# Two key heads joined into one attention item, and the softmax scale folded into the transposes

## The chip, the cores and the metric

The kernel runs on one core of a Trainium2 chip. The metric is the device time of one execution in microseconds (us). Everything is float32.

## The reference, cut to what matters

The reference is a chain of three transformer blocks over 512 tokens of width 1024: a gated delta net, a retention block, and a block whose mixer is half HGRN2 and half a sparse attention, each followed by a convolutional feed-forward layer. Only the sparse attention (`nsa`) is touched. It has 8 query heads in 2 key heads (groups) of 4, each 64 wide. Every query head attends over three branches and the results are summed with a gate for each:

```
s     = einsum(q, k_cmp) * scale                   # branch 0: 31 compressed keys
p_cmp = softmax(where(cvalid, s, NEG)) * any_valid
o_cmp = p_cmp @ v_cmp
o_slc = softmax(causal(q @ k_s * scale)) @ v_s     # branch 1
o_win = softmax(causal(q @ k_w * scale)) @ v_w     # branch 2
o     = g0 * o_cmp + g1 * o_slc + g2 * o_win
```

With 512 tokens all 8 blocks are selected and the window covers everything, so branches 1 and 2 are plain causal attention over 512 keys.

## The kernel before, in words

The program is one straight-line list of instructions for each engine (TensorE, VectorE, ScalarE, GpSimd), ordered by hand. Every engine counts its finished steps in one semaphore, and another engine waits until that count has reached the number of a named step (`at("act", "nsa", "exp", n)`); there is no planner. Activations are held transposed: features on the 128 partitions, tokens along the free axis. Weights come through a ring of three slots filled by the SyncE queue; the attention stage below reads none of them.

The attention stage is written in `pe_nsa`, `act_nsa` and `dve_nsa`. Its queries lie in `NX[half(g), r, :]`: key head g = 0 on partitions 0-63 and g = 1 on 64-127, four query heads r in each. The work after the compression is a list of 72 items `ITEMS = (r, g, b, i)`: for each of 4 r and 2 g, one item of the compressed branch (b = 0, all 4 blocks of 128 queries at once) and four each of branches 1 and 2, one per block i of 128 queries, which sees (i+1)*128 keys. An item goes round the engines:

- TensorE, `scores` (L1936 for b = 0, L1939 else): queries (64 rows by 128) as weights, keys streamed, into one of four banks in rotation, up to 3 items ahead.
- VectorE, `front` (L2068 to L2071, or L2074): mask, and the maximum of each row. For b > 0 one instruction and a read of its accumulator.
- ScalarE, `exp` (L2002, L2004): the exponential into `Pn`, for b > 0 with the row sum.
- VectorE (L2087 to L2092, or L2095 and L2097): the reciprocal, then the whole row times reciprocal times gate. L2097 writes (i+1)*128 columns.
- TensorE (L1969): one transpose per 128 keys, into bank 2 or 3.
- ScalarE (L2016, L2018): the copy of that bank into `PTn`.
- TensorE, `values` (L1951, L1954): `VSW` or `VCMP` (128 or 31 rows by 64 columns) as weights, `PTn` streamed, into `O[half(g)]`, partitions 0-63 or 64-127 of one bank for each r, where the three branches add up.

In TensorE's queue the order within one turn n is `scores(n+3)`, transposes of n, `values(n-1)`. VectorE does `front(n+1)` before the scaling of n, and ScalarE `exp(n+1)` before the copy of n. When the 9 items of a head pair are done, `dve_o` (L2117) copies the bank into `HT`. A float32 matmul is two passes through the array (two MATMUL instructions, each with its own weight load); a transpose is one. After the stage comes `mix_out` (L267), a projection with weights already in the ring.

Of the kernel before, what the change touches and what calls it, by code (L numbers as in the profile page):

```python
# [7 lines left out]
ALU = mybir.AluOpType  # L8
# [78 lines left out]
def program(nc, dr, out, plan):  # L87
# [3 lines left out]
    with ExitStack() as ctx:  # L91
# [22 lines left out]
        def at(*name):  # L114
            return plan.get(name, 1)
# [1750 lines left out]
        o = work + 6 * T  # L1866
        KCMP = region(o, 32); o += 32
        VCMP = region(o, 2, ND); o += 2 * ND
        assert o <= 21504
        Pn = [region(work + m * T, T) for m in range(3)]  # L1870
        PTn = [region(work + (3 + m) * T, T) for m in range(2)]
        tri = region(work + 5 * T, T)
        SB = (0, 1, 6, 7)
# [3 lines left out]
        ITEMS = [(r, g, b, i) for r in range(4) for g in range(NG) for b, i in [(0, 0)] + [(b, i) for b in (1, 2) for i in range(NT)]]  # L1877

        def half(g):
            return slice(ND * g, ND * g + ND)  # L1880

        def pe_nsa(pe):
# [47 lines left out]
            def scores(n):  # L1930
                r, g, b, i = ITEMS[n]
                if n >= 4:
                    pe.wait_ge(act_done, at("act", "nsa", "exp", n - 4))
                if b == 0:
                    for i in range(NT):
                        last = nc.tensor.matmul(B4[SB[n % 4]][:, i, 0:NCMP], NX[half(g), r, i * P:(i + 1) * P], KCMP[half(g), 0:NCMP],  # L1936
                                                start=True, stop=True)
                else:
                    last = nc.tensor.matmul(B[SB[n % 4]][:, 0:(i + 1) * P], NX[half(g), r, i * P:(i + 1) * P],  # L1939
                                            NX[half(g), 5 + b, 0:(i + 1) * P], start=True, stop=True)  # L1940
                last.then_inc(pe_done, PE.tick("nsa", "score", n))

            def values(n):

                r, g, b, i = ITEMS[n]
                pe.wait_ge(act_done, at("act", "nsa", "pt", n))
                O = B[4 + r % 2]
                if b == 0:
                    if g == 0 and r >= 2:
                        pe.wait_ge(dve_done, at("dve", "nsa", "o", r - 2))  # L1950
                    last = nc.tensor.matmul(O[half(g), :], VCMP[0:NCMP, g, :], PTn[n % 2][0:NCMP, :], start=True, stop=True)  # L1951
                else:
                    for j in range(i + 1):
                        last = nc.tensor.matmul(O[half(g), i * P:(i + 1) * P], VSW[:, j, (b - 1) * P + g * ND:(b - 1) * P + (g + 1) * ND],  # L1954
                                                tiles(PTn[n % 2])[:, j, :], start=False, stop=True, skip_group_check=True)
                last.then_inc(pe_done, PE.tick("nsa", "pv", n))
# [3 lines left out]
            scores(2)  # L1960
            for n, (r, g, b, i) in enumerate(ITEMS):
                if n + 3 < len(ITEMS):
                    scores(n + 3)
                pe.wait_ge(dve_done, at("dve", "nsa", "p", n))
                if n >= 2:
                    pe.wait_ge(act_done, at("act", "nsa", "pt", n - 2))
                p4 = tiles(Pn[n % 3])
                for j in range(NT if b == 0 else i + 1):
                    last = nc.tensor.transpose(B4[2 + n % 2][:, j, :], p4[:, j, :], ident[:, :])  # L1969
                last.then_inc(pe_done, PE.tick("nsa", "pt", n))  # L1970
                if n:
                    values(n - 1)
# [3 lines left out]
        def act_nsa(act):  # L1976
# [19 lines left out]
            def exp(n):  # L1996
                r, g, b, i = ITEMS[n]
                act.wait_ge(dve_done, at("dve", "nsa", "max", n))
                if n >= 3:
                    act.wait_ge(pe_done, at("pe", "nsa", "pt", n - 3))  # L2000
                if b == 0:
                    ins = nc.scalar.activation(tiles(Pn[n % 3])[:, :, 0:NCMP], B4[SB[n % 4]][:, :, 0:NCMP], ACT.Exp, scale=SCALE)  # L2002
                else:
                    ins = nc.scalar.activation(Pn[n % 3][:, 0:(i + 1) * P], B[SB[n % 4]][:, 0:(i + 1) * P], ACT.Exp, scale=-1.0,  # L2004
                                               bias=small[:, 20 + n % 3:21 + n % 3], accum_out=small[:, 40 + n % 3:41 + n % 3])
                ins.then_inc(act_done, AC.tick("nsa", "exp", n))

            exp(0)
            for n, (r, g, b, i) in enumerate(ITEMS):
                if n + 1 < len(ITEMS):  # L2010
                    exp(n + 1)
                act.wait_ge(pe_done, at("pe", "nsa", "pt", n))
                if n >= 2:
                    act.wait_ge(pe_done, at("pe", "nsa", "pv", n - 2))
                if b == 0:
                    ins = nc.scalar.activation(PTn[n % 2][0:NCMP, :], B[2 + n % 2][0:NCMP, :], ACT.Copy)  # L2016
                else:
                    ins = nc.scalar.activation(PTn[n % 2][:, 0:(i + 1) * P], B[2 + n % 2][:, 0:(i + 1) * P], ACT.Copy)  # L2018
                ins.then_inc(act_done, AC.tick("nsa", "pt", n))
            AC.mark("end", "nsa")  # L2020

        def dve_nsa(dve):
# [29 lines left out]
            for m in range(3):  # L2052

                nc.vector.memset(Pn[m], 0.0).then_inc(dve_done, DV.tick())
# [3 lines left out]
            cm = cmask[:, :, 0:NCMP]  # L2058

            def front(n):  # L2060

                r, g, b, i = ITEMS[n]
                dve.wait_ge(pe_done, at("pe", "nsa", "score", n))
                if n >= 3:
                    dve.wait_ge(act_done, at("act", "nsa", "exp", n - 3))
                if b == 0:
                    S = B4[SB[n % 4]][:, :, 0:NCMP]
                    step(nc.vector.tensor_tensor(S, S, cm, ALU.add))  # L2068
                    step(nc.vector.reduce_max(small[:, 24:28], S, AX))
                    m4 = small[:, 24:28].rearrange("p (i o) -> p i o", o=1).to_broadcast([P, NT, NCMP])  # L2070
                    nc.vector.tensor_tensor(S, S, m4, ALU.subtract).then_inc(dve_done, DV.tick("nsa", "max", n))  # L2071
                else:
                    S = B[SB[n % 4]]
                    nc.vector.tensor_tensor_reduce(out=S[:, 0:(i + 1) * P], in0=S[:, 0:(i + 1) * P], in1=tri[:, (3 - i) * P:4 * P],  # L2074
                                                   scale=-SCALE, scalar=3e38, op0=ALU.add, op1=ALU.min,
                                                   accum_out=small[:, 20 + n % 3:21 + n % 3]).then_inc(dve_done, DV.tick("nsa", "max", n))

            front(0)
            for n, (r, g, b, i) in enumerate(ITEMS):
                if n + 1 < len(ITEMS):  # L2080
                    front(n + 1)
                dve.wait_ge(act_done, at("act", "nsa", "exp", n))
                head = NG * 2 * g + r
                if b == 0:
                    Pc = tiles(Pn[n % 3])[:, :, 0:NCMP]
                    s4 = small[:, 32:36]
                    step(nc.vector.reduce_sum(s4, Pc, AX))  # L2087
                    step(nc.vector.reciprocal(s4, s4))
                    step(nc.vector.tensor_tensor(s4, s4, cmask[:, :, 31:32].rearrange("p i o -> p (i o)"), ALU.mult))
                    step(nc.vector.tensor_tensor(s4, s4, VSW[:, :, 256 + 3 * head], ALU.mult))  # L2090
                    w4 = s4.rearrange("p (i o) -> p i o", o=1).to_broadcast([P, NT, NCMP])
                    nc.vector.tensor_tensor(Pc, Pc, w4, ALU.mult).then_inc(dve_done, DV.tick("nsa", "p", n))  # L2092
                else:
                    s = small[:, 36 + n % 2:37 + n % 2]
                    step(nc.vector.reciprocal(s, small[:, 40 + n % 3:41 + n % 3]))  # L2095

                    nc.vector.tensor_scalar(Pn[n % 3][:, 0:(i + 1) * P], Pn[n % 3][:, 0:(i + 1) * P], s,  # L2097
                                            VSW[:, i, 256 + 3 * head + b:257 + 3 * head + b], ALU.mult, ALU.mult)\
                        .then_inc(dve_done, DV.tick("nsa", "p", n))
                if g == 1 and b == 0 and r:  # L2100
                    dve_o(dve, r - 1)
# [11 lines left out]
        def dve_o(dve, r):  # L2113

            last_item = max(n for n, item in enumerate(ITEMS) if item[0] == r)
            dve.wait_ge(pe_done, at("pe", "nsa", "pv", last_item))
            nc.vector.tensor_copy(HT[:, 4 + r, :], B[4 + r % 2][:, :]).then_inc(dve_done, DV.tick("nsa", "o", r))  # L2117
# [342 lines left out]
```

## Time and profile before

| | us |
|---|---|
| median of 3 runs | 3148.64 (3146.46 to 3150.63) |
| the profiled execution | 3151.16 |
| its span, first to last instruction | 3149.3 |
| TensorE busy in the span | 2975.5 (94%) |
| VectorE, ScalarE busy | 1561.0, 643.6 |
| mean granted TensorE clock | 0.934 |

Lines of code are named L1939 and so on. A group of the profile is all instructions of one line, engine and shape, with its busy time, the mean duration of one, and the idle time of the engine before them. A granted clock of 1.00 is 2.4 GHz for TensorE, 0.50 is 1.2 GHz. A matmul's record is longer than the time for which it holds the array, since one begins before the record of the last one ends; so the distance from start to start is what counts.

### The profile page before, as it was taken

The page shows a single profiled execution, that of the slowest core. Times are in us where ns is not written, and L with a number is a line of the kernel's source. Part 1 is how long each engine was busy: PE and PEld are TensorE (multiplying, and loading weights), DVE is VectorE, ACT ScalarE, POOL GpSimd, SP SyncE. Part 2 cuts the span into 40 slices and gives each one's busy share as a digit, 9 for nine tenths or more (in the row PEclk, how much of TensorE's full clock was granted, in tenths as well). Part 3 has the DMA queues.
Part 4 walks back from the last instruction along what each step waited for, and adds up shares of the span by engine and source line. Part 5 has one row for each costly group of instructions (what it writes and reads, how often), then busy time and mean ns, then how long its engine had stood idle before and what let it go on. Part 6 is the DMA issues. An engine that isn't in the chain of part 4 may idle for free. (4 is left out here: it accounts for less than half of the span.)

```text
span 3149.3 us, 29504 instructions
## 1 busy us (share of the span) xinstructions
PE 2975.5 (94%) x11724; PEld 2053.1 (65%) x11724; DVE 1561.0 (50%) x2776; ACT 643.6 (20%) x1124; POOL 149.6 (5%) x118
## 2 busy tenths in 40 slices
PE   6999999889999999999899999979998999999999
PEld 5666666648888854444346888854454555488888
DVE  3555565537777520222116776646564333366652
ACT  1112211112111010111102111024535222122200
POOL 0000000001000010000001000001230000000000
PEclk9998999899999999999899999989998555999999
DMA  7112111122443321211122444320113000122221
GB/s 291 37 58 89 67 54 54 54 80 107 164 176 125 138 90 54 84 57 57 53 80 80 167 178 146 128 90 30 68 54 134 1 1 1 54 81 80 91 92 46
DMA packets 24488, 274.96 MB, mean 87 GB/s; under 512 B 3480, under 2 KB 4376, under 8 KB 7072
## 3 DMA queue, kind: packets, MB, share of 16 engines
q1 hardware_dynamic: 19440, 266.45, 22.8%
q10 hardware_dynamic: 4912, 6.63, 0.6%
q8 instruction: 94, 1.54, 0.2%
q14 instruction: 42, 0.34, 0.0%
HBM read 270.97 MB, written 2.10 MB: 87 GB/s over the span
## 5 line engine op out<-in xcount | busy, mean ns | idle before, releaser
L323 PE MATMUL bank<-HT,ring 128*128 128x256 f32 x1056 | 257.7, 389 | 20.1 <-ACT HT L671 12.7
L939 PE MATMUL bank<-HT,ring 128*128 128x512 f32 x512 | 261.0, 640 | 0.0
L323 PE MATMUL bank<-arena 128*128 128x256 f32 x1056 | 249.5, 379 | 0.0
L323 PE MATMUL bank<-arena,ring 128*128 128x256 f32 x1056 | 249.5, 379 | 0.0
L323 PEld LDWEIGHTS bank<-HT,ring 128*128 128x128 f32 x1056 | 204.1, 195 | 51.7 <-issue 23.3
L323 PEld LDWEIGHTS bank<-arena 128*128 128x128 f32 x1056 | 200.6, 190 | 27.3
L323 PEld LDWEIGHTS bank<-arena,ring 128*128 128x128 f32 x1056 | 200.6, 190 | 27.3
L400 PE MATMUL bank<-arena,ring 128*128 128x256 f32 x936 | 207.5, 380 | 5.5 <-ACT arena L470 3.9
L267 PE MATMUL bank<-arena,ring 128*128 128x512 f32 x448 | 198.2, 602 | 10.3 <-issue 7.9
L400 PEld LDWEIGHTS bank<-arena,ring 128*128 128x128 f32 x936 | 177.0, 190 | 30.9 <-ACT arena L470 5.1
L244 DVE SCALAR_TENSOR_TENSOR arena<-ring,evec,arena 128x512 f32<-128x512 f32 x224 | 167.3, 747 | 3.8
L267 PEld LDWEIGHTS bank<-arena,ring 128*128 128x128 f32 x448 | 86.5, 194 | 120.5 <-issue 119.4
L1535 PE MATMUL bank<-HT,ring 128*128 128x512 f32 x320 | 148.1, 600 | 4.3 <-ACT HT L699 4.3
L860 ACT ACTIVATE arena<-bank,ffc 128x512 f32<-128x512 f32 x66 | 51.3, 777 | 471.3 <-DVE bank L788 471.3
L939 PEld LDWEIGHTS bank<-HT,ring 128*128 128x128 f32 x512 | 95.4, 205 | 79.0 <-issue 79.0
L323 PE MATMUL bank<-HT,arena 128*128 128x256 f32 x528 | 126.4, 382 | 0.2
L1355 PE MATMUL bank<-ring,HT 128*128 128x512 f32 x256 | 114.7, 608 | 8.2 <-ACT arena L660 8.2
L1336 PE MATMUL bank<-HT,ring 128*128 128x512 f32 x256 | 112.9, 602 | 6.3 <-ACT HT L671 6.3
L400 PE MATMUL bank<-arena 128*128 128x256 f32 x528 | 116.4, 379 | 0.0
L1369 PE MATMUL bank<-HT,ring 128*128 128x512 f32 x256 | 110.5, 592 | 0.0
L323 PEld LDWEIGHTS bank<-HT,arena 128*128 128x128 f32 x528 | 98.6, 190 | 18.2 <-DVE arena L838 5.7
L400 PEld LDWEIGHTS bank<-arena 128*128 128x128 f32 x528 | 100.3, 190 | 13.6
(395 smaller groups left out, 4203.8 us busy)
## 6 DMA issues: line engine op xcount, KB each, us to landing
ring<-w_ada SPq DMA_DIRECT2D x33, 2048.0 KB, 8.0
ring<-w_up SPq DMA_DIRECT2D x33, 2048.0 KB, 7.8
ring<-w_down SPq DMA_DIRECT2D x24, 1408.0 KB, 6.0
ring<-w_gdn SPq DMA_DIRECT2D x8, 2048.0 KB, 12.4
ring<-w_ret_qk SPq DMA_DIRECT2D x4, 2048.0 KB, 8.0
ring<-w_ret_v SPq DMA_DIRECT2D x4, 2048.0 KB, 7.9
ring<-w_ret_g SPq DMA_DIRECT2D x4, 2048.0 KB, 7.8
ring<-w_ret_out SPq DMA_DIRECT2D x4, 2048.0 KB, 7.9
```

What stands on the lines that cost most here:

```text
L244: ins = nc.vector.scalar_tensor_tensor(out=acc, in0=w[:, :, k, :], scalar=evec[:, e, k:k + 1], in1=acc, op0=ALU.mult, op1=ALU.add)
L267: last = nc.tensor.matmul(bank[:, :], w[:, n % per_load, k, :], src(k), start=(k == 0), stop=(k == kc - 1))
L323: last = nc.tensor.matmul(out_, w[:, k, :], x[:, k, :], start=(first and k == 0), stop=(k == 3), skip_group_check=not first)
L400: last = nc.tensor.matmul(out_, w[:, k, :], x(k), start=(first and k == 0), stop=(k == KH2 - 1), skip_group_check=not first)
L860: nc.scalar.activation(ffn_y[:, j % 2, :], B[j % 2][:, :], ACT.Identity, scale=ffc[:, i, j, 0, 2:3], bias=ffc[:, i, j, 0, 3:4])\
L939: last = nc.tensor.matmul(B[u % 2][:, :], w[:, u, k, :], HT[:, k, :], start=(k == 0), stop=(k == KC - 1))
L1336: last = nc.tensor.matmul(B[X + u][:, :], w[:, u, k, :], HT[:, k, :], start=(k == 0), stop=(k == KC - 1))
L1355: last = nc.tensor.matmul(B[Y + i][:, :], HT[:, k, i * P:(i + 1) * P], w[:, k, :], start=(k == 0), stop=(k == KC - 1))
L1369: last = nc.tensor.matmul(B[Y + u][:, :], w[:, u, k, :], HT[:, k, :], start=(k == 0), stop=(k == KC - 1))
L1535: last = nc.tensor.matmul(bank[:, :], w[:, u, k, :], HT[:, k, :], start=(k == 0), stop=(k == KC - 1))
```

## The change: what it does

Items become `(r, b, i)`, 36 of them, each for both key heads. Scores of the two heads are issued one after the other from rows 0-63 and 64-127 into two banks, up to 2 items ahead; two pairs of banks alternate. The values of the two heads are issued alternately into bank 4, partitions 0-63, and bank 5, partitions 64-127, and these two banks now serve every r. For b > 0 VectorE no longer scales the rows of `Pn`: it scales the identity (128 by 128) by reciprocal times gate into one of six tiles `scale_n`, and TensorE multiplies `Pn` by that diagonal matrix instead of transposing it, which transposes and scales at once. The copies into `PTn`, the exponentials and the maxima stay one instruction per key head. `dve_o` copies two halves of 64 partitions.

```diff
-        SB = (0, 1, 6, 7)
+        scale_n = [region(o + m * P, P) for m in range(6)]; o += 6 * P
+        SB = ((0, 1), (6, 7))
-        ITEMS = [(r, g, b, i) for r in range(4) for g in range(NG) for b, i in [(0, 0)] + ...]
+        ITEMS = [(r, b, i) for r in range(4) for b, i in [(0, 0)] + ...]
...
             def scores(n):
-                if n >= 4:
-                    pe.wait_ge(act_done, at("act", "nsa", "exp", n - 4))
+                if n >= 2:
+                    pe.wait_ge(act_done, at("act", "nsa", "exp", n - 2, 1))
...
+                    for g in range(NG):
+                        last = nc.tensor.matmul(B[SB[n % 2][g]][:, 0:(i + 1) * P], NX[half(g), r, i * P:(i + 1) * P],
+                                                NX[half(g), 5 + b, 0:(i + 1) * P], start=True, stop=True)
...
             def values(n):
+                pe.wait_ge(act_done, at("act", "nsa", "pt", n, 1))
                 if b == 0:
+                    if r:
+                        pe.wait_ge(dve_done, at("dve", "nsa", "o", r - 1))
...
                     for j in range(i + 1):
+                        for g in range(NG):
+                            last = nc.tensor.matmul(B[4 + g][half(g), i * P:(i + 1) * P], VSW[:, j, (b - 1) * P + g * ND:(b - 1) * P + (g + 1) * ND],
+                                                    PTn[n % 2][:, g, j * P:(j + 1) * P], start=False, stop=True, skip_group_check=True)
...
+            for n, (r, b, i) in enumerate(ITEMS):
+                if n + 2 < len(ITEMS):
+                    scores(n + 2)
+                for g in range(NG):
+                    pe.wait_ge(dve_done, at("dve", "nsa", "p", n, g))
+                    if n:
+                        pe.wait_ge(act_done, at("act", "nsa", "pt", n - 1, g))
+                    for j in range(NT if b == 0 else i + 1):
+                        if b == 0:
+                            last = nc.tensor.transpose(B4[2 + g][:, j, :], Pn[n % 3][:, 4 * g + j, :], ident[:, :])
+                        else:
+                            last = nc.tensor.matmul(B4[2 + g][:, j, :], Pn[n % 3][:, 4 * g + j, :], scale_n[2 * (n % 3) + g], start=True, stop=True)
...
# VectorE, after the exponentials
+                dve.wait_ge(act_done, at("act", "nsa", "exp", n, 1))
...
-                    nc.vector.tensor_scalar(Pn[n % 3][:, 0:(i + 1) * P], Pn[n % 3][:, 0:(i + 1) * P], s,
-                                            VSW[:, i, 256 + 3 * head + b:257 + 3 * head + b], ALU.mult, ALU.mult)
+                    step(nc.vector.reciprocal(small[:, c:c + 2], small[:, c:c + 2]))
+                    for g in range(NG):
+                        nc.vector.tensor_scalar(scale_n[2 * (n % 3) + g], ident[:, :], small[:, c + g:c + g + 1],
+                                                VSW[:, i, 256 + 3 * head + b:257 + 3 * head + b], ALU.mult, ALU.mult)
...
-            nc.vector.tensor_copy(HT[:, 4 + r, :], B[4 + r % 2][:, :])
+            nc.vector.tensor_copy(HT[half(0), 4 + r, :], B[4][half(0), :])
+            nc.vector.tensor_copy(HT[half(1), 4 + r, :], B[5][half(1), :])
```

## Rows read from the trace of the kernel before

**Rows 1.** The page: granted clock of TensorE in 40 equal slices, in tenths.
```profile
PEclk9998999899999999999899999989998555999999
```
**Rows 2.** Stretches: length, busy us (count) of each engine, clock, DMA share, GB/s.
```profile
2434.00:2679.00 245.00, 243.47 (x721) 137.16 (x721) 90.89 (x325) 68.24 (x211) 0.00 (x0) 0.52 0.01 3
```
**Rows 3.** Groups of 2434.2 to 2679.5 by shape, TensorE's matmuls.
```profile
L1954 PE MATMUL bank<-arena 128*64 128x128 f32 x320 | 82.4, 422 | 0.0
L1969 PE MATMUL bank<-ident,arena 128*128 128x128 f32 x192 | 58.1, 430 | 0.2 <-DVE arena L2097 0.2
...
L1939 PE MATMUL bank<-arena 64*128 64x512 f32 x32 | 31.9, 1096 | 0.0
...
L1936 PE MATMUL bank<-arena 64*128 64x31 f32 x64 | 15.3, 400 | 0.4 <-ACT arena L1993 0.4
```
**Rows 4.** Timeline at the low clock: start, length, engine, line, operation, count.
```profile
2453.35 2.07 PE L1939 MATMUL bank<-arena 64*128 64x512 f32 x2
...
2455.35 0.47 PE L1969 MATMUL bank<-ident,arena 128*128 128x128 f32 x1
...
2455.75 1.97 PE L1954 MATMUL bank<-arena 128*64 128x128 f32 x8
...
2457.65 1.91 PE L1936 MATMUL bank<-arena 64*128 64x31 f32 x8
...
2459.50 0.69 PE L1969 MATMUL bank<-ident,arena 128*128 128x128 f32 x2
```
**Rows 5.** Timeline of TensorE where shapes alternate and nothing is waited for.
```profile
2432.15 0.64 PE L1925 MATMUL bank<-w2c,arena 128*31 128x64 f32 x4
2432.72 0.64 PE L1923 MATMUL bank<-arena,w2c 128*64 128x31 f32 x4
```
**Rows 6.** Timeline of TensorE about the first rise of the clock.
```profile
2500.13 1.11 PE L1969 MATMUL bank<-ident,arena 128*128 128x128 f32 x4
2501.17 1.97 PE L1954 MATMUL bank<-arena 128*64 128x128 f32 x8
...
2504.64 1.07 PE L1951 MATMUL bank<-arena 31*64 31x512 f32 x2
2505.64 0.48 PE L1939 MATMUL bank<-arena 64*128 64x128 f32 x2
2506.05 0.44 PE L1969 MATMUL bank<-ident,arena 128*128 128x128 f32 x2
2506.42 0.43 PE L1954 MATMUL bank<-arena 128*64 128x128 f32 x2
2506.78 1.00 PE L1939 MATMUL bank<-arena 64*128 64x256 f32 x2
```
**Rows 7.** Stretches before, in and after that rise, and one of the delta net.
```profile
2500.20:2503.60 3.40, 3.40 (x13) 2.71 (x14) 1.20 (x4) 1.03 (x3) 0.00 (x0) 0.50 0.00 0
2503.80:2507.00 3.20, 3.20 (x12) 1.23 (x11) 1.67 (x6) 1.31 (x5) 0.00 (x0) 1.00 0.00 0
2507.20:2510.60 3.40, 3.40 (x11) 1.72 (x9) 1.62 (x6) 1.22 (x5) 0.00 (x0) 0.50 0.00 0
...
600.00:626.00 26.00, 19.63 (x151) 17.54 (x149) 21.34 (x40) 0.65 (x2) 0.10 (x1) 1.00 0.01 2
```
**Rows 8.** Group of 600 to 626, TensorE: the stretch's products.
```profile
L1026 PE MATMUL bank<-arena 128*128 128x128 f32 x48 | 6.4, 277 | 0.8 <-DVE arena L1251 0.8
```
**Rows 9.** Timeline of TensorE at the stage's end, after the last scores.
```profile
2671.11 1.97 PE L1954 MATMUL bank<-arena 128*64 128x128 f32 x8
...
2674.73 0.65 PE L1954 MATMUL bank<-arena 128*64 128x128 f32 x4
```
**Rows 10.** Groups of VectorE and ScalarE, 2434.2 to 2679.5.
```profile
L2074 DVE CUSTOM_DVE_ANT_0 bank<-bank,arena 128x512 f32<-128x512 f32 x16 | 11.2, 699 | 28.9 <-PE bank L1939 28.9
L2004 ACT ACTIVATE arena<-bank,small 128x512 f32<-128x512 f32 x16 | 10.9, 681 | 0.0
...
L2097 DVE TENSOR_SCALAR arena<-arena,small 128x128 f32<-128x128 f32 x16 | 5.5, 346 | 0.6
```

More of the change, by code:

```diff
@@ L1865, in program @@
         assert o <= 4 * HH * T
-        o = work + 6 * T
+        o = work
+        Pn = [region(o + m * 2 * T, 2 * NT, P) for m in range(3)]; o += 6 * T
+        PTn = [region(o + m * 2 * T, 2, T) for m in range(2)]; o += 4 * T
+        tri = region(o, T); o += T
         KCMP = region(o, 32); o += 32
         VCMP = region(o, 2, ND); o += 2 * ND
[L1869 to L1872, printed above, removed]
-        SB = (0, 1, 6, 7)
+        scale_n = [region(o + m * P, P) for m in range(6)]; o += 6 * P
+        assert o <= 26000, o
+        SB = ((0, 1), (6, 7))
         NORMED = [4, 0, 1, 2, 3, 6, 7]
@@ L1876, in program @@
         SCALE = ND ** -0.5
[L1877 removed]
+        ITEMS = [(r, b, i) for r in range(4) for b, i in [(0, 0)] + [(b, i) for b in (1, 2) for i in range(NT)]]
         def half(g):
@@ L1959, in pe_nsa @@
             scores(1)
[L1960 to L1970, printed above, removed]
+            for n, (r, b, i) in enumerate(ITEMS):
+                if n + 2 < len(ITEMS):
+                    scores(n + 2)
+                for g in range(NG):
+                    pe.wait_ge(dve_done, at("dve", "nsa", "p", n, g))
[6 more added lines that the diff above has]
+                            last = nc.tensor.matmul(B4[2 + g][:, j, :], Pn[n % 3][:, 4 * g + j, :], scale_n[2 * (n % 3) + g], start=True, stop=True)
+                    last.then_inc(pe_done, PE.tick("nsa", "pt", n, g))
                 if n:
@@ new lines, in front @@
+                    S = [B4[SB[n % 2][g]][:, :, 0:NCMP] for g in range(NG)]
+                    m4 = [small[:, 24 + 4 * g:28 + 4 * g] for g in range(NG)]
+                    for g in range(NG):
+                        ins = nc.vector.tensor_tensor(S[g], S[g], cm, ALU.add)
+                    step(ins)
+                    for g in range(NG):
+                        ins = nc.vector.reduce_max(m4[g], S[g], AX)
+                    step(ins)
+                    for g in range(NG):
+                        nc.vector.tensor_tensor(S[g], S[g], m4[g].rearrange("p (i o) -> p i o", o=1).to_broadcast([P, NT, NCMP]), ALU.subtract)\
+                            .then_inc(dve_done, DV.tick("nsa", "max", n, g))
+                else:
+                    for g in range(NG):
+                        S, c = B[SB[n % 2][g]], 2 * (n % 2) + g
+                        nc.vector.tensor_tensor_reduce(out=S[:, 0:(i + 1) * P], in0=S[:, 0:(i + 1) * P], in1=tri[:, (3 - i) * P:4 * P],
+                                                       scale=-SCALE, scalar=3e38, op0=ALU.add, op1=ALU.min,
+                                                       accum_out=small[:, 20 + c:21 + c]).then_inc(dve_done, DV.tick("nsa", "max", n, g))
@@ L2078, in dve_nsa @@
             front(0)
[L2079 removed]
+            for n, (r, b, i) in enumerate(ITEMS):
                 if n + 1 < len(ITEMS):
                     front(n + 1)
[L2082 to L2083 removed]
+                dve.wait_ge(act_done, at("act", "nsa", "exp", n, 1))
                 if b == 0:
[L2085 to L2092, printed above, removed]
[L2093 to L2100 removed]
@@ new lines, in dve_nsa @@
+                    Pc = Pn[n % 3][:, :, 0:NCMP]
+                    s8 = small[:, 32:40]
+                    step(nc.vector.reduce_sum(s8, Pc, AX))
+                    step(nc.vector.reciprocal(s8, s8))
+                    for g in range(NG):
+                        s4 = s8[:, 4 * g:4 * g + 4]
+                        step(nc.vector.tensor_tensor(s4, s4, valid, ALU.mult))
+                        step(nc.vector.tensor_tensor(s4, s4, VSW[:, :, 256 + 3 * (NG * 2 * g + r)], ALU.mult))
+                        w4 = s4.rearrange("p (i o) -> p i o", o=1).to_broadcast([P, NT, NCMP])
+                        nc.vector.tensor_tensor(Pc[:, 4 * g:4 * g + 4, :], Pc[:, 4 * g:4 * g + 4, :], w4, ALU.mult)\
+                            .then_inc(dve_done, DV.tick("nsa", "p", n, g))
+                else:
+                    c = 40 + 2 * (n % 2)
+                    step(nc.vector.reciprocal(small[:, c:c + 2], small[:, c:c + 2]))
+                    for g in range(NG):
+                        head = NG * 2 * g + r
+                        nc.vector.tensor_scalar(scale_n[2 * (n % 3) + g], ident[:, :], small[:, c + g:c + g + 1], VSW[:, i, 256 + 3 * head + b:257 + 3 * head + b],
+                                                ALU.mult, ALU.mult).then_inc(dve_done, DV.tick("nsa", "p", n, g))
@@ L2101, in dve_nsa @@
+                if b == 1 and i == 0 and r:
                     dve_o(dve, r - 1)
```

70 lines of the change are left out of this document (29 added, 41 removed).

## The prediction, made before the changed kernel ran

> **What bounds the kernel now.** I read four views in this order. First the page: TensorE is busy 94% of the span (the table above), and its granted clock is near full except in three of the 40 slices, where it is about a half [rows 1]. Those slices are the attention stage. Second the stage as one stretch: in the 245 us from 2434 to 2679 TensorE is busy 243.5, VectorE 90.9, ScalarE 68.2, the DMA engines nearly nothing, and the clock stands at 0.52 [rows 2]. So TensorE bounds the stage, at 1.2 GHz, and a wait of another engine costs nothing as long as TensorE has other work. Third the groups, which give counts: 320 value passes, 192 transposes, 128 score passes (32 of each width), 64 and 16 passes of the compressed branch [rows 3]. Fourth the timeline of single items, which gives prices.
>
> Price of a pass, at the low clock. One transpose takes 0.47 and two 0.69, eight value passes 1.97 [rows 4]: (1.97 - 0.47) / 7 = 0.214 us for each further pass of 128 columns. I call that a unit; 512 columns are four units. At the high clock two passes take 0.43 [rows 6] and four 0.65 [rows 9]: a unit is 0.11. A record's rest is a tail that overlaps what follows.
>
> Price of a change of shape, from start to start. One transpose to the values behind it: 0.40 - 0.21 = 0.19. Eight value passes to the scores: 1.90 - 1.71 = 0.19. Score passes of 512 to the transpose: 2.00 - 1.71 = 0.29 [rows 4]. That is 0.67 us for each item, which goes round scores, transposes, values. It is not the price of a wait: where shapes alternate and nothing is waited for, four passes of 64 columns (0.43) take 0.57 until the next shape begins [rows 5]. At the high clock the three are 0.19, 0.15 and 0.14 [rows 6]: 0.48.
>
> Does this add up to the stage? The 64 items of branches 1 and 2 hold 320 units of scores, 320 of values, 160 of transposes: 800 x 0.214 = 171. Changes: 64 x 0.67 = 43. A compressed item costs 1.85 (its eight score passes, start to start [rows 4]) + 0.86 + 1.71 + 0.38 for two changes = 4.8, and 8 of them 38. Sum 252 for 245 measured; the stretches in which the clock was up [rows 7, 9] make up the difference.
>
> **The change part by part.** What it does to TensorE is counted in units, since it is the bound.
>
> Scores. Each key head's two passes stay, on half of the rows. If the two halves run side by side, head 0's second pass lies beside head 1's first, and a pair costs three passes where it cost four: 240 units for 320. If not, 320. The trace before never has two half-height or half-width tiles next to each other without another shape between, so both ends stay; I take the overlap, since the two use different rows and banks.
>
> Values. The two heads alternate, each on 64 columns of its own bank: 2(i+1)+1 passes for 4(i+1) if side by side, 192 units for 320. If not, 320. I take the overlap for the same reason; the side that costs stays in the range. The Trainium skill (TensorEngine Tiling (Array Packing), Key Properties) states that different tiles run in parallel and that changing the tiling mode drains the engine. The second half agrees with the 0.19 to 0.29 above; no run here shows the first.
>
> Transposes. 160 one-pass transposes become 160 two-pass products: 320 units for 160. This is a loss for certain, unless it buys something else.
>
> Changes of shape. 36 items for 72. The second key head's transposes wait for two more semaphores, but in the same shape. In the old trace waiting weight loads in one shape cost nothing visible when their count was reached long before, so I price them at nothing; at the other end they cost a change each, 36 x 0.19 = 7 us. What is queued behind them is the values of n-1, and ScalarE's copies wait for those products.
>
> Compressed items: 16 score passes that load weights more than they stream, 1.85 x 2 = 3.7 at the low clock (I assume that the halves save nothing here; at best half), 8 transposes, and 12 units of values (16 without overlap).
>
> VectorE. The rescaling of whole rows (16 each of 0.35 to 0.55, 28.6 us by the four shapes) becomes 64 tiles of 128 columns at 0.346 [rows 10] = 22.1. 32 reciprocals go, at 0.16 each, 5 us; the halved copies `dve_o` double, 4 x 0.69 more, and 0.7 of it is exposed at the end. VectorE stays near 82 us, ScalarE at 68. The three memsets of `Pn` are twice as long, some 1.6 us, before the first maximum, beside the first two scores; if that cover is gone it costs 1.6.
>
> Sum at the low clock: 240 + 192 + 320 = 752 units x 0.214 = 161; changes 32 x 0.67 = 21; compressed items 4 x (3.7 + 1.7 + 2.6 + 0.5) = 34. That is 216, 29 us less than 245. Without overlap it is 960 x 0.214 + 21 + 4 x 9.3 = 264, 19 us more.
>
> **The clock.** This term is larger than all the others. TensorE is busy without a gap, and still at 1.2 GHz. So the trace shows that being busy is not what brings the high clock; I looked at what ran before it changed. The first rise, just after 2503.6, follows four transposes and eight value passes, all on 128 rows [rows 6, 7]. It lasts some 3.4 us, in which 31-row and 64-row passes run [rows 6], and by 2507.2 the clock is down again [rows 7]. At the stage's end, once no scores are left and only values and transposes run, it is up too: four value passes take 0.65 there, where eight took 1.97 just before [rows 9]. Elsewhere, products of 128x128x128 on all rows hold 1.00 over 26 us in which TensorE is busy just 19.6 [rows 7, 8]. What keeps this stage at the low clock is then its share of passes on half of the rows, 320 of 800 units, and the changes between shapes.
>
> The change moves both. Transposes are 320 of its units, values 192 to 320, all on 128 rows; scores fall to 240, in a third of which both halves are at work; and half of the changes go. I take it that the clock rises within the first few items and, since full-height work at twice the speed held it elsewhere with a quarter of the time idle, stays.
>
> Sum at the high clock: 752 x 0.11 = 83; changes 32 x 0.48 = 15; compressed items 4 x (1.9 + 0.9 + 1.3 + 0.3) = 18 with rounding up for weight loads. That is 116. To it: the first items at the low clock, 10 us instead of 5, +5; a fall at the compressed items, whose scores and values stream 31 columns or rows, +1 each, +4; and waits. TensorE now needs some 116 us where VectorE needs 82 and its small gaps, so it is covered less. The chain from a pair's scores to its products is two maxima of 0.70, an exponential of 0.68, its sum, a reciprocal and two tiles of 0.35 [rows 10], about 3.3 us, against two turns of TensorE work, 1.6 us each for one block and 4.6 for four. It is exposed after short items only: I take 8 for the 36 items. With the 0.7 at the end: 134.
>
> The stage goes from 245 to 134: -111. The profiled execution, 3151.2, becomes 3040; it lies 2.5 above the median of the runs, so the median becomes 3038.
>
> The Trainium skill (TensorE: Matmul & The Clock Gate, Part 4: PE-mode transpose) says that transposes do not bring the high clock. The trace agrees only in part: the rise after 2503.6 came behind four transposes and eight value passes, and whether the values alone did it cannot be read. By that rule replacing transposes with products is what matters, and the sum would be the same 134.
>
> **The rivals.**
>
> Overlap fails, clock rises. 960 units x 0.11 = 106, + 15 + 4 x 4.8 = 140, + 18 = 158: median 3062. For it: no row shows two halves at once. Against: they share neither rows nor banks, or neither columns nor banks.
>
> The clock swings. The compressed items and the waits pull it down for part of each head, say four tenths of the stage: between 134 and 216, near 170: 3074. For it: the fall by 2507.2 came with 31- and 64-row passes [rows 6, 7]. Against: that was one short run of them.
>
> The clock stays low, halves overlap: 216, 3120. For it: the stage stands at 0.52 now, and the scores remain on half rows.
>
> The slower one: the clock stays low and the halves run one after the other, so the second pass of each of the 160 products is paid in full. 264 us, +19: 3168. If each change of half costs as much as a change of shape (32 + 28 in the scores, 132 in the values, 192 x 0.19 = 36), 300 us: 3203. The second passes cost 160 x 0.214 = 34 us and fewer changes give back 24 (36 x 0.67), so it decides from the point at which the overlap gives less than 10 of the 45 us (208 units) that I count for it. Rows 5 speak for it, since width changes there cost time without a wait; against it, that is another shape, not another half of one.
>
> That the change doesn't do what it says (run halves side by side) is the first rival and this last one.
>
> **How the numbers follow.** Forecast (high clock, overlap) 0.58; high clock without overlap 0.14; swinging clock 0.10; low with overlap 0.08; low without, slower, 0.08; no change within 0.2% 0.02, where losses and gains meet. What a measurement of this kernel can tell from no change is about 0.2%, 6 us. Faster 0.90, same 0.02, slower 0.08. The time is the forecast's, 3038. Its own bounds: waits and falls at nothing (118 + 5) give 3025, twice what I took gives 3055. The range holds these, the case without overlap and the swinging clock: 3020 to 3105.
>
> **What would show it.** Right: the stage about 134 us long; its clock over 0.9 after the first 10 us; 752 units, so that starts of the two heads' passes coincide; L1939's second head begins before the first head's second pass ends; the L1969 products twice as many and 0.11 apart; VectorE busy near 82. Wrong: the clock at 0.50 in the products; records of the two heads end to end; TensorE idle behind VectorE for more than a tenth of the stage, or a changed stage after 2679.

## The result, and the profile after

The changed kernel takes 3016.17 us (median of 4 runs, 3010.99 to 3020.42), the kernel before 3149.64 beside it: a ratio of 0.9577, with a 95% interval of 0.9556 to 0.9598. A second measurement of the same kernel on another occasion gave 3016.32 and again 0.9577 (0.9557 to 0.9598). The forecast was 3038 with a range of 3020 to 3105: right in direction, cause and order of size, but the gain was 133 us and not 111, and the time lies 4 us below the range. (Of the four runs the profiled one took 3012.24, some 4 us under the median; the stage below is read from it.)

The page of the changed kernel: the span, the busy time, and the granted clock in 40 slices. The three slices at a half of before [rows 1] are gone.

```profile
span 3010.4 us, 29648 instructions
...
PE 2834.6 (94%) x11884; PEld 1993.0 (66%) x11884; DVE 1542.0 (51%) x2740; ACT 642.8 (21%) x1124; POOL 149.6 (5%) x118
...
PEclk9999999899999999999989999999899999999999
```

The stage runs from its first score at 2432.0 to the first pass of the projection at 2539.7. As stretches (length, then busy time and count of TensorE, its weight loads, VectorE, ScalarE, GpSimd; clock; DMA), whole, its first 10 us, and the rest without its end:

```profile
2432.00:2539.70 107.70, 103.57 (x880) 74.77 (x880) 71.72 (x291) 67.15 (x209) 0.00 (x0) 0.96 0.01 5
2432.00:2442.00 10.00, 8.36 (x44) 5.50 (x44) 7.77 (x34) 5.61 (x18) 0.00 (x0) 0.60 0.10 43
2442.00:2534.00 92.00, 91.11 (x792) 65.83 (x792) 62.58 (x256) 60.06 (x191) 0.00 (x0) 1.00 0.01 2
```

It was 244.6 us at a clock of 0.52 [rows 2, between the same two passes]. That is 137 us less, and the spans differ by 139; from the stage's end to the last instruction the two take 470 us each. The whole gain lies in the stage. TensorE still bounds it: it is busy 91 of 92 us, at the full clock.

TensorE's groups in the stage by shape (count, busy us, mean ns; idle before). They answer to [rows 3]: the products are twice the passes, the others are as many as before but are busy for less than a third of the time.

```profile
L1976 PE MATMUL bank<-arena 128*128 128x128 f32 x320 | 44.2, 285 | 0.6 <-DVE arena L2120 0.5
L1959 PE MATMUL bank<-arena 128*64 128x128 f32 x320 | 24.4, 283 | 0.0
L1943 PE MATMUL bank<-arena 64*128 64x512 f32 x32 | 9.0, 641 | 0.0
```

The timeline of TensorE (start, length, line, shape, count), in which the passes of both heads stand in one row:

```profile
2473.21 2.05 PE L1976 MATMUL bank<-arena 128*128 128x128 f32 x16
2475.19 0.88 PE L1959 MATMUL bank<-arena 128*64 128x128 f32 x12
2476.00 0.92 PE L1943 MATMUL bank<-arena 64*128 64x384 f32 x4
2476.84 0.71 PE L1976 MATMUL bank<-arena 128*128 128x128 f32 x4
2477.49 1.09 PE L1959 MATMUL bank<-arena 128*64 128x128 f32 x16
2478.51 1.13 PE L1943 MATMUL bank<-arena 64*128 64x512 f32 x4
```

Sixteen value passes take 1.09 us, twelve 0.88 and, elsewhere in the stage, four 0.44: (1.09 - 0.88) / 4 = 0.053 for a further pass, half of 0.11. Both heads' passes run all the way side by side. In the single records the first two passes of every such group start 6 to 8 ns apart, in the values and in the scores, and the third 0.16 us or more later. Passes of one half never start so close together (0.109 us apart, in the run with grouped values below), so each of these pairs is one pass of head 0 and one of head 1. The four score passes of 512 columns take 1.13, where two took 2.07 at the low clock [rows 4]. The sixteen products take 2.05, at 0.11 each.

### The profile page after: what moved, and what is told of

Read it like the earlier page. It is cut to its first block and busy times, and to the rows that moved or that the text cites. A ratio compares the mean times of both kernels' runs of the same rounds, so it can differ in the third digit from the quotient of the medians.

```text
span 3010.4 us, 29648 instructions
## 1 busy us (share of the span) xinstructions
PE 2834.6 (94%) x11884; PEld 1993.0 (66%) x11884; DVE 1542.0 (51%) x2740; ACT 642.8 (21%) x1124; POOL 149.6 (5%) x118
## 5 line engine op out<-in xcount | busy, mean ns | idle before, releaser
L323 PE MATMUL bank<-HT,ring 128*128 128x256 f32 x1056 | 258.1, 390 | 20.1 <-ACT HT L671 12.7
L400 PEld LDWEIGHTS bank<-arena 128*128 128x128 f32 x528 | 100.3, 190 | 13.6
```

The lines of the kernel that those rows point to most:

```text
L323: last = nc.tensor.matmul(out_, w[:, k, :], x[:, k, :], start=(first and k == 0), stop=(k == 3), skip_group_check=not first)
L400: last = nc.tensor.matmul(out_, w[:, k, :], x(k), start=(first and k == 0), stop=(k == KH2 - 1), skip_group_check=not first)
```

## The experiments

Stage lengths are from the first score pass to the first pass of the projection, in the profiled execution. The part of the program ahead of the stage differs by up to 8 us from one profiled execution to another, while the stage of two kernels that were profiled twice came out the same within 0.1 us, so the stage is the finer measure. In the executions shown the clock falls 1 to 3 us before the stage begins. The fifth column is the length of that first stretch at the low clock, the last one all the time at the low clock within the stage.

| kernel | time, us | ratio to before | stage, us | first low stretch, us | low in the stage, us |
|---|---|---|---|---|---|
| before | 3149 | 1 | 244.6 | 72 | 233 |
| changed | 3016 | 0.9577 | 107.7 | 10 | 8 |
| one half at a time | 3091 | 0.983 | 182.9 | 38 | 63 |
| values grouped | 3015 | 0.959 | 113.9 | 10 | 9 |
| joined, transposes | 2998 | 0.954 | 95.0 | 10 | 8 |
| one head, product | 3083 | 0.980 | 184.8 | 44 | 53 |
| one head, scores on all rows | 3038 | 0.964 | 134.5 | 10 | 8 |
| scores one half at a time | 3057 | 0.970 | 158.0 | 34 | 63 |
| joined, transposes, interleaved | 3002 | 0.953 | 96.6 | 10 | 7 |
| joined, transposes, split wait | 3006 | 0.954 | 97.0 | 10 | 8 |

**One head per item, scores on all 128 rows.** This is the kernel before; only the keys lie in tiles whose other half is zero, so that a score pass uses all rows.

```diff
-    last = nc.tensor.matmul(B[SB[n % 4]][:, 0:(i + 1) * P], NX[half(g), r, i * P:(i + 1) * P],
-                            NX[half(g), 5 + b, 0:(i + 1) * P], start=True, stop=True)
+    last = nc.tensor.matmul(B[SB[n % 4]][:, 0:(i + 1) * P], NX[:, r, i * P:(i + 1) * P],
+                            KZ[:, 2 * g + b - 1, 0:(i + 1) * P], start=True, stop=True)
...
+    ins = nc.vector.tensor_copy(KZ[half(g), 2 * g + b - 1, :], NX[half(g), 5 + b, :])
...
+    ins = nc.gpsimd.memset(KZ[half(1 - g), 2 * g:2 * g + 2, :], 0.0)
```

> The kernel before, one key head per item, plain transposes; the scores of branches 1 and 2 run over all 128 rows, queries of both heads against a key tile whose other half is zero (same result, same number of passes and of columns; four half copies on VectorE, 3 us, and zeros from GpSimd). Theory (the passes on half of the rows are what keeps the clock low): it rises within 10 to 40 us and stays; 800 units x 0.11 + 64 items at about 0.35 for changes (scores and transposes now have one shape) + 8 compressed items at 3 = 135, and up to 20 for the start and waits: stage 140 to 160 us, time 3045 to 3065. Rival (it is the mere mix of short groups, or the transposes): clock near 0.5, only the changes save, 64 x 0.2 = 13 us, about 3140.

Measured: 3037.89 us, ratio 0.9637 (0.9621 to 0.9654). Its stage as stretches:

```profile
2428.50:2563.00 134.50, 133.07 (x720) 86.17 (x720) 89.10 (x328) 67.96 (x210) 0.00 (x0) 0.97 0.01 4
2436.50:2560.00 123.50, 123.00 (x684) 79.44 (x683) 82.50 (x305) 64.03 (x200) 0.00 (x0) 1.00 0.00 1
```

The same 720 matmuls as before, none shared, no product and no joining, and the stage falls from 245 to 134.5 us: 110 of the 137. The clock reads 1.00 from 2436.5 on. The edit also takes away one change of shape in three, since scores and transposes now have the same; at the low clock that is at most 64 x 0.29 = 19 us [rows 4]. The rest, 91 us, is the clock. The theory stands, and the run did better than it gave: the stage is 5 us below its 140 to 160, the time 7 us below its 3045 to 3065, and the clock was up after 8 us where it gave 10 to 40. The run doesn't fill the rows alone, since that one change of shape goes with it; what the changes of shape do for the clock is taken up below.

**One head per item, diagonal product.** The kernel before with only the product put in, for branches 1 and 2; the compressed branch keeps its transposes.

```diff
...
-    last = nc.tensor.transpose(B4[2 + n % 2][:, j, :], p4[:, j, :], ident[:, :])
+    last = nc.tensor.matmul(B4[2 + n % 2][:, j, :], p4[:, j, :], scale_n[n % 3], start=True, stop=True)   # b > 0
...
-    nc.vector.tensor_scalar(Pn[n % 3][:, 0:(i + 1) * P], Pn[n % 3][:, 0:(i + 1) * P], s,
+    nc.vector.tensor_scalar(scale_n[n % 3], ident[:, :], s,
...
```

> The kernel before, items of one key head, with only the diagonal product in place of scaling the rows and transposing. Theory (passes on all rows lift the clock, and the 160 more units are such): clock rises in the first items and stays, 960 units x 0.11 + 64 changes at 0.48 + 8 compressed items at about 3 = 160 to 175 us, time about 3070. Rival (it takes the joined halves to lift the clock): clock near 0.5, 245 + 34 = about 279 us, time about 3183.

Measured: 3082.53 us, ratio 0.980 (0.976 to 0.984). The stage up to the rise, then two stretches behind it:

```profile
2432.30:2475.30 43.00, 42.97 (x129) 27.84 (x130) 14.65 (x59) 11.34 (x33) 0.00 (x0) 0.50 0.03 14
2475.40:2598.20 122.80, 122.80 (x671) 79.94 (x670) 64.61 (x249) 50.69 (x159) 0.00 (x0) 1.00 0.00 1
...
2598.30:2608.50 10.20, 10.20 (x34) 6.81 (x33) 2.67 (x11) 2.94 (x9) 0.00 (x0) 0.50 0.00 1
```

160 passes more than before, nothing shared, and still 66 us faster. TensorE works without a gap in both stretches: 129 matmuls in the 43 us at the low clock, 671 in 122.8 at the high one, 3.0 and 5.5 in a us. The clock came, as the theory said, but after 43 us and not in the first items, and it fell once more for 10 us, so the stage was 185 us, not 160 to 175.

**Joined items, plain transposes.** The changed kernel with the scale put back on the rows.

```diff
-    last = nc.tensor.matmul(B4[2 + g][:, j, :], Pn[n % 3][:, 4 * g + j, :], scale_n[2 * (n % 3) + g], start=True, stop=True)
+    last = nc.tensor.transpose(B4[2 + g][:, j, :], Pn[n % 3][:, 4 * g + j, :], ident[:, :])
...
-    nc.vector.tensor_scalar(scale_n[2 * (n % 3) + g], ident[:, :], small[:, c + g:c + g + 1],
+    row = Pn[n % 3][:, 4 * g:4 * g + i + 1, :].rearrange("p j c -> p (j c)")
+    nc.vector.tensor_scalar(row, row, small[:, c + g:c + g + 1],
...
```

> Joined items as in the change, but the scale put on the rows by VectorE and plain one-pass transposes on TensorE as before the change. Theory (what lifts the clock is passes on all 128 rows, transposes among them, two halves at once counting as all rows): clock over 0.9, 160 units fewer on TensorE (-17.6 us), VectorE 9 us more and a longer wait for it, stage between 93 and 108, time 3001 to 3016. Rival (the product, being no transpose, is what lifts the clock): clock near 0.5, 480 units x 0.214 + 21 for changes + 25 for compressed items = about 149, time about 3057.

Measured: 2998.45 us, ratio 0.9536 (0.9508 to 0.9563). Its stage, and who waits in it (in total, times, longest):

```profile
2433.30:2528.30 95.00, 85.03 (x721) 53.44 (x721) 76.70 (x291) 65.16 (x209) 0.00 (x0) 0.96 0.02 6
2441.50:2520.00 78.50, 72.89 (x630) 44.60 (x626) 65.48 (x251) 57.26 (x190) 0.00 (x0) 1.00 0.01 1
```

```profile
PEld bank L1973 <- DVE arena L2118: 14.9, 23, 1.3
...
PE bank L1973 <- DVE arena L2118: 5.3, 8, 1.1
```

The clock is high without a single product, so the product is not needed to lift it. The stage lies within the 93 to 108 us of the theory, the time 3 us below its 3001. With the product the stage is 12.7 us longer than with the transposes it replaced: with transposes TensorE is busy 18.5 us less, but idle for 10.0 us and not 4.1, since it waits more for VectorE, which is busy 5 us more. This kernel is the fastest tried, so it was measured again beside the changed one.

> Joined items with one-pass transposes and VectorE scaling the rows, once more. Theory (the product's 160 second passes are 17.6 us of TensorE, of which VectorE's longer scaling gives 5 back): 12 to 13 us less than the changed kernel beside it (stage 95 against 108), about 3003. Rival (the difference of the first runs was the chip's): within 5 us of it.

> The changed kernel once more, beside the joined items with transposes, on one chip. Expected: 0.9577 of the kernel before, as first measured, about 3016, stage 108 us. If the time swings by more than 5 us between chips, the difference to the other one is what counts.

Measured: 2999.90 (2995.53 to 3007.57) with transposes and 3016.32 (3009.49 to 3018.25) for the changed kernel; the ratios are 0.9532 (0.9510 to 0.9554) and 0.9577 (0.9557 to 0.9598), the stages 95.0 and 107.8. 16 us less at the median, 13 in the stage.

**One half at a time.** Head 1's passes wait for the end of head 0's, in scores and values of branches 1 and 2.

```diff
     last = nc.tensor.matmul(B[SB[n % 2][g]][:, 0:(i + 1) * P], NX[half(g), r, i * P:(i + 1) * P],
                             NX[half(g), 5 + b, 0:(i + 1) * P], start=True, stop=True)
+    if g == 0:
+        last.then_inc(pe_done, PE.tick("nsa", "half"))
+        pe.wait_ge(pe_done, PE.n)
...
-    for j in range(i + 1):          # values
-        for g in range(NG):
+    for g in range(NG):
+        for j in range(i + 1):
...
+        if g == 0:                  # the same wait after head 0
...
```

> The changed kernel, but TensorE waits for head 0's passes to end before it issues head 1's, in the scores and in the values of branches 1 and 2 (values grouped by head). Theory (the two heads truly share the array, which makes 160 units of each pass count instead of 320): 320 units more at 0.11 us = 35, and 64 waits for the end of a half at about 0.35 each = 22, so the stage goes from 108 to about 165 us and the time from 3016 to about 3073. Rival (the gain is the clock and the fewer changes of shape, the overlap is worth little): the waits alone, 22, about 3038. Both expect the high clock.

Measured: 3090.67 us, ratio 0.983 (0.979 to 0.986), 75 us more than the changed kernel where 57 were expected; the stage is 75.2 us longer. The waits cost less than their price: at the high clock head 1's first pass starts 0.33 us after a last pass of 128 columns and 0.65 after one of 512, 0.21 more than a pass that follows at once, so 64 of them are 14 us and not 22. What the expectation left out is the clock, which it had left high:

```profile
2427.90:2464.00 36.10, 35.06 (x110) 21.52 (x110) 13.20 (x56) 11.77 (x36) 0.00 (x0) 0.50 0.04 15
2464.00:2528.80 64.80, 63.23 (x377) 41.35 (x375) 30.09 (x123) 26.61 (x87) 0.00 (x0) 1.00 0.00 1
2528.90:2542.50 13.60, 13.37 (x40) 8.17 (x40) 3.42 (x15) 4.12 (x14) 0.00 (x0) 0.50 0.00 0
```

It stayed low for 36 us and fell twice more, 13.6 us each time: 63 us of the stage against 8 in the changed kernel. Work at the low clock takes about twice as long, so 55 us more of it cost an estimated 27, and 35 + 14 + 27 = 76 is what was measured. Sharing the array does two things, then: it halves the passes and it keeps all rows at work.

**Scores one half at a time.** The same wait in the scores alone; the values still share.

> The changed kernel, with head 1's scores alone waiting for head 0's to end (values still share). Theory (both heads' first passes start together, so sharing saves half of 320 units, not a quarter): 160 units more, 17.6 us, and 32 waits at about 0.4, 13 us, so +31 us, about 3047, if the clock stays high; up to 15 us more if it falls for longer at the start. Rival (sharing saves a quarter, 80 units, as the prediction had it): 9 + 13 = +22 us, 3038. The trace tells them apart by the starts.

Measured: 3057.40 us in two runs, ratio 0.970 (0.968 to 0.972), so 41 us more than the changed kernel, the stage 50 us longer. That is more than both prices gave, and again it is the clock: it was low for the first 32 us of the stage and three times in all, 63 us together (the third stretch, of 13.7 us, isn't shown).

```profile
2430.70:2462.90 32.20, 31.28 (x102) 18.86 (x103) 13.06 (x56) 10.60 (x32) 0.00 (x0) 0.50 0.04 15
...
2486.90:2503.80 16.90, 16.79 (x71) 12.46 (x70) 4.75 (x21) 5.88 (x18) 0.00 (x0) 0.50 0.00 1
```

With what the runs measured, the size speaks for the half. A wait costs 0.21 here too, not 0.4, so 32 of them are 7 us, and the 55 us more at the low clock some 27, as above. With 160 units (17.6 us) that gives 52, with 80 units 43; the stage is 50.3 us longer. The starts in the changed kernel, 6 to 8 ns apart from the first pass on, say the same without an estimate.

This run and the one before it spend the same 63 us at the low clock, though the values share the array here and not there. So it is the scores one half of the rows at a time that cost the clock; values on all rows and one half of the columns at a time didn't add to it.

**Values grouped by head.** The two loops of the values change places, nothing else.

```diff
-    for j in range(i + 1):
-        for g in range(NG):
+    for g in range(NG):
+        for j in range(i + 1):
```

> The changed kernel with the values issued head by head (all blocks of head 0, then all of head 1) and not alternately, no wait added. If TensorE starts passes in the order of issue, as the prediction had it, only one pass of each item is shared: 4(i+1)-1 instead of 2(i+1) passes, 128 units more, +14 us, about 3030. If its queue can take head 1's passes ahead of head 0's by any distance, nothing changes: 3016. A short look-ahead (two or three passes) gives a value between, near the first.

Measured: 3015.13 us, ratio 0.9589 (0.9562 to 0.9616), no different from the changed kernel; the stage is 6.2 us longer. Its value passes:

```profile
2473.81 1.14 PE L1959 MATMUL bank<-arena 128*64 128x128 f32 x12
...
2476.37 1.58 PE L1959 MATMUL bank<-arena 128*64 128x128 f32 x16
```

Sixteen passes take 1.58 where they took 1.09 alternating and would take 1.97 or so one by one (sixteen at 0.11 and the tail). Head 1's first pass starts 0.49 us after head 0's first, when five of its eight have started. Where head 0 has six passes it starts when three have started, and where it has four or two, behind the first. So the engine doesn't start passes in the order of issue: it takes one for the other half ahead, over three passes at most in this kernel. The third expectation is the nearest: the stage's +6 lies between 0 and 14, if not near the upper end.

**Two orders of VectorE, on top of the joined items with transposes.** Interleaved: maximum of head 0 of the next item, scaling of head 0, maximum of head 1, scaling of head 1 (where neither item is compressed), and each scaling waits for its own exponential and has its own reciprocal.

> Joined items with transposes (the earlier experiment, stage 95 us, TensorE idle 20 us behind VectorE's scaling). VectorE's order changed: maximum of head 0 of the next item, scaling of head 0, maximum of head 1, scaling of head 1. Theory (the scaling comes late because two maxima of up to 0.7 stand ahead of it and it waits for both exponentials): up to 10 of the 20 us come back, less 5 us of VectorE for 32 more reciprocals that now stand where it has slack: 2990 to 2998. Rival (VectorE's and ScalarE's own work fills the loop): no change or 5 us slower, 2998 to 3004.

Split wait: the order kept, each head's scaling waiting for its own exponential alone. The cut below is against the joined items with transposes.

```diff
-    dve.wait_ge(act_done, at("act", "nsa", "exp", n, 1))
-    step(nc.vector.reciprocal(small[:, c:c + 2], small[:, c:c + 2]))
     for g in range(NG):
+        dve.wait_ge(act_done, at("act", "nsa", "exp", n, g))
+        step(nc.vector.reciprocal(small[:, c + g:c + g + 1], small[:, c + g:c + g + 1]))
...
```

> Joined items with transposes, VectorE's order kept, but the scaling of head 0 waits for head 0's exponential alone and not for both, at the price of 32 more reciprocals of 0.16 (5 us of VectorE). Theory (waiting for the second exponential delays the first transposes by about 0.7 on the longer items): 3 to 8 us less, 2990 to 2996. Rival (VectorE gets to the scaling after both exponentials anyway, since two maxima stand ahead): the reciprocals alone, 0 to 5 us more, 2998 to 3004.

Measured: 3001.89 us, 0.9527 (0.9510 to 0.9545), stage 96.6; and 3006.27 us, 0.9537 (0.9520 to 0.9554), stage 97.0. Neither helps. With the order interleaved TensorE's weight loads wait for the scaling as long as before (15.2 us against 14.9), and so do its matmuls (5.8 against 5.3):

```profile
PEld bank L1973 <- DVE arena L2124: 15.2, 28, 0.9
```

The rivals hold by the stage, 1.6 and 2.0 us longer where they gave 0 to 5; the time with the split wait is 2 us above the 3004 of its rival, with a ratio that can't be told from the kernel without it. Both expectations hoped to win back part of 20 us of waiting. That is the waits of the weight loads and of the matmuls added up, while TensorE as a whole is idle for 10.0 of the 95 us. With transposes VectorE (77 of 95 us busy) and ScalarE (65) are close behind TensorE (85), and neither order gives anything back.

## Why the prediction was right or wrong

**What bounds the stage.** Right. TensorE at the low clock before, TensorE at the high clock after; VectorE, busy 72 us (82 forecast), and ScalarE, busy 67 (68 forecast), lie below it. VectorE's work was forecast well all the same: its records add up to 98.2 us before and 89.2 after, 9 us less as forecast. Busy time fell by more because neighbouring records, now of two heads, overlap and are counted once there.

**The clock, the largest term.** Right in direction, and its ground held up. Scores on all rows, alone, bring the high clock after 8 us and the stage to 134.5. Over all runs the line is clean: where score passes of 64 rows run alone (before; one head with the product; the two with halves one at a time) the clock stays low for 34 to 72 us at the start and falls again later, and where all 128 rows are at work in the scores (changed, grouped, transposes, zero-filled keys) it is low for 7 to 10 us and stays up. The prediction had named the changes of shape beside the rows. Fewer of them is not enough: one half at a time has 96 in its items of branches 1 and 2 and spends 63 us at the low clock, while one head with scores on all rows has 128 and spends 8. That they play no part at all isn't shown, for no run fills the rows and leaves every change. Why the clock rises at all, late, where score passes of 64 rows still run alone, stays open too. One step of the argument was weaker than I wrote: it counted the products among what lifts the clock. They help where items aren't joined (one head with the product), but the joined items don't need them.

**The rule on transposes.** The prediction weighed what the Trainium skill (TensorE: Matmul & The Clock Gate, Part 4: PE-mode transpose) says, that transposes don't bring the high clock. The joined items with transposes are at 1.00 from 2441.5 to 2520, with 192 transposes among the 720 matmuls of the stage, a larger part in time than in the kernel before (29 of 95 us, start to start, against 53 of 245). They did not hold the clock down; whether they alone could raise it no run shows.

**Sharing the array: the step that failed, with the waits below.** The mechanism was right, its size was not. The prediction had "a pair costs three passes where it cost four" and "2(i+1)+1 passes for 4(i+1)". I supposed that head 1's first pass has to wait until head 0's second has begun, because it stands behind it in the queue. It starts with head 0's first. (The prediction's own sign, "752 units, so that starts of the two heads' passes coincide", joined two things that don't go together: passes whose starts coincide from the first on come to 640.) So the units are 160 for the scores and 160 for the values, not 240 and 192: 112 x 0.11 = 12 us too many. By itself that would have made the forecast 3026 and not 3038, still 10 us above the measurement; the rest is in the next two terms.

**The compressed items.** Forecast 18; start to start their scores take 4.8, transposes 5.0 and values 4.0 in all, 13.8, the first at the low clock included. That weight loads gain nothing from the halves was the wrong assumption: 16 of them take 1.92 at the low clock, where 8 took 1.91 [rows 4].

```profile
2432.03 1.92 PE L1939 MATMUL bank<-arena 64*128 64x31 f32 x16 [0.43 <-ACT arena L2000]
```

**Falls, start and waits.** Forecast 5 + 4 + 8 + 0.7 = 18. The clock did not fall once after 2442, so 4 were not due. Of TensorE's waits the longest in the changed kernel are those of weight loads, for VectorE's scaling (7.7 us in all) and for ScalarE's copies (4.3), and most of that lies under passes that still run; TensorE as a whole is idle 4.1 of 107.7 us. Counted another way, the passes of branches 1 and 2 and all between them take 94 us from start to start. Units are 640 x 0.11 = 70, changes 32 x 0.55 = 18 (0.20 before values, 0.15 before scores and 0.20 before products, from the starts in the timeline above), so some 6 us are left for waits and the start, where 18 were forecast. This term missed by as much as the sharing did. Forecast minus measured: 12 for sharing, 4 for the compressed items, 12 for start, falls and waits, less 2 because a change costs 0.55 and not 0.48: 26, the whole of 134 - 108. The medians differ by 22 only, since the profiled execution lies 4 us below its kernel's median.

**The product.** "A loss for certain, unless it buys something else" was right, and in the joined items it bought nothing: it costs 12.7 us of the stage. The prediction never asked whether joining would bring the clock without it.

**The changes of shape, the second head's waits, VectorE.** Right: 36 products' waits in the same shape cost nothing visible, since the second head's products follow at 0.11. VectorE's scaling is all recorded: 64 tiles of 0.344 are 22.0 us, where 22.1 were forecast and the rows took 28.6. The 19.3 busy us of this group are less because the records of an item's two tiles overlap.

```profile
L2120 DVE TENSOR_SCALAR arena<-ident,small,arena 128x128 f32<-128x128 f32 x64 | 19.3, 344 | 1.3
```

**The slower rival.** Its mechanism, no sharing and twice the transposes, was built in the run with one half at a time: 3091, not 3168 to 3203, because the clock rose there as well; it is low for 63 of the 183 us.

**The range.** Its low end came from dropping all waits while holding on to three passes for a pair. (It was worked out as 118 + 5, where the sum above it gives 116 + 5 + 0.7, a difference of 1 us.) The overlap was priced at both ends for failure only, never for working better than in order.

## What to carry to other kernels

Where TensorE is busy all the time and the granted clock stands at a half, look at which passes use only part of the rows. Filling the other half, even with zeros and for no useful work, was worth 91 to 110 us of a 245 us stage here, more than everything else in the change. Two matmuls on different row halves or column halves and in different banks took the time of one here when they were issued next to each other; issued eight passes apart, part of that was lost. And a one-pass transpose should not be given up for a two-pass product where TensorE is the bound; whether it pays where VectorE is, no run here shows.

## What the runs showed of the hardware

- Two-pass float32 matmuls on two halves start 6 to 8 ns apart, head 1's first pass ahead of head 0's second. Issued in two blocks of eight, the second block starts 0.49 us late, ahead of the last three passes of the first block.
- A semaphore wait for the end of the other half's passes costs 0.21 us at the high clock and 0.26 at the low one, beyond a pass that follows at once (one half at a time).
- With one head per item and the product, TensorE got through 3.0 matmuls a us in its first 43 us, at the low clock, and 5.5 in the 123 us behind them, at the high one, busy without a gap in both. Busy time shows nothing of the clock.
- A change of shape costs 0.14 to 0.20 us at the high clock; a change of half within one shape costs nothing that the starts show (6 to 8 ns).
